# A hybrid decoder layer on one core: sample-scan products laid between z products, sample sequences as attention units, the last conv tap on ScalarE, the last down tiles block by block

## What is computed

```python
h = rms_norm(x); z, xBC, dt, q, k, v, g1, g2 = split(h @ w_in)
u = silu(causal_conv4(xBC)); y = ssd_scan(u, dt, state) * silu(z)        # 32 heads of 64, 8 groups, state 128
A = group_norm(y) @ w_ssm_out;  B = window_attention_with_sinks(rope(q), rope(k), v) @ w_attn_out
x = x + (sigmoid(g1) * A + sigmoid(g2) * B) @ w_out
x = x + peer(rms_norm(x))     # 16384 experts, 8 heads, top 16: sum of gate * gelu(h . u_e) * v_e
y = rms_norm(x)               # also: new conv rows, new scan states, new k and v windows
```

## Time and profile before

| | us |
|---|---|
| median of 3 runs | 2764.11 (2760.47 to 2771.31) |
| the profiled execution | 2769.13 |
| its span | 2767.3 |
| conv stage, middle | 60.0 to 249.5 |
| sample scan with z tiles | 398.4 to 614.1 |
| prompt attention | 694.4 to 824.1 |
| sample attention | 824.1 to 875.4 |
| down tiles | 2010.0 to 2740.7 |
| behind the last down tile | 2740.7 to 2767.3 |

### The profile page before, as it was taken

The page is one execution under the profiler, slowest core; times in us unless marked ns, Lnnn a source line. Parts: engine busy times, 40 slices in busy tenths (PEclk is TensorE's granted clock), DMA queues, the critical chain, the costliest instruction groups (busy, mean ns, idle before and its releaser), DMA issues.

```text
span 2767.3 us, 45108 instructions
## 1 busy us (share of the span) xinstructions
PE 2539.8 (92%) x14964; PEld 2329.5 (84%) x14964; DVE 1932.9 (70%) x3510; ACT 1032.8 (37%) x1975; POOL 963.6 (35%) x540
## 2 busy tenths in 40 slices
PE   6999679999768999989999998998998999999997
PEld 5998469999436999979988888888898999999996
DVE  5998864543663752238899998888566888888876
ACT  2332752226332532113333387787332222222221
POOL 1333353323000333324445565656432222222221
PEclk9999887899886999989999999999999999999999
DMA  3222243332001222313334478788899999999994
GB/s 128 70 81 70 87 137 105 113 116 79 28 6 31 68 77 83 106 52 115 122 130 142 142 260 295 258 316 298 322 315 311 311 308 312 313 304 312 312 302 150
DMA packets 264994, 490.31 MB, mean 177 GB/s; under 512 B 137249, under 2 KB 172833, under 8 KB 263713
## 3 DMA queue, kind: packets, MB, share of 16 engines
q1 hardware_dynamic: 67408, 222.85, 23.7%
q10 hardware_dynamic: 160624, 132.00, 14.7%
q0 software_dynamic: 36864, 134.23, 13.8%
HBM read 417.59 MB, written 73.39 MB: 177 GB/s over the span
## 4 chain that ended last, share of the span: by engine, by line
PE 38%; DVE 8%; DMA 3%; ACT 3%; issue 2%; POOL 1%; ACTq 1%; DVEq 0%; SPq 0%
PE ps L1132 23%; PE ps L1031 11%; PE ps L654 2%; DMA raw<-wt 2%; PE ps L1102 1%; DMA row<-pu,row_idx 1%; DVE onehot_pick L2173 1%; POOL wlo L565 1%; ACT rinv L1553 1%; DVE onehot_pick L2170 1%; DVE expert_parts L2176 1%; ACT g_block L1572 1%; ACT whi L1197 1%; ACT onehot_i L1557 1%; DVE pick L2150 0%
## 5 line engine op out<-in xcount | busy, mean ns | idle before, releaser
L565 POOL TENSOR_TENSOR wlo<-raw,whi 128x1024 fp32r<-128x1024 f32 x215 | 547.1, 2545 | 1077.5 <-ACT whi L1197 1077.3
L1197 ACT ACTIVATE whi<-raw 128x1024 fp32r<-128x1024 f32 x373 | 394.5, 1058 | 1346.0 <-PE ps L1132 461.0
L1031 PE MATMUL ps<-h_hi,whi 128*128 128x448 f32 x1024 | 382.3, 373 | 15.9 <-POOL wlo L565 10.8
L1132 PE MATMUL ps<-act_hi,whi 128*128 128x448 f32 x1024 | 374.8, 366 | 8.7 <-DVE act_lo L1643 8.7
L1031 PE MATMUL ps<-h_lo,whi 128*128 128x448 f32 x1024 | 378.4, 370 | 0.0
L1031 PE MATMUL ps<-h_hi,wlo 128*128 128x448 f32 x1024 | 377.9, 369 | 0.0
L1132 PE MATMUL ps<-act_lo,whi 128*128 128x448 f32 x1024 | 374.6, 366 | 0.0
L1132 PE MATMUL ps<-act_hi,wlo 128*128 128x448 f32 x1024 | 374.6, 366 | 0.0
L572 POOL DMA_INDIRECT row<-pv,row_idx x128 | 163.0, 1273 | 471.6 <-DVE row_acc L2253 459.7
L2246 DVE TENSOR_TENSOR wlo<-raw,whi 128x1024 fp32r<-128x1024 f32 x158 | 193.7, 1226 | 130.0 <-ACT whi L1197 122.3
L654 PE MATMUL ps<-h_hi,whi 128*128 128x288 f32 x1104 | 249.1, 308 | 27.6 <-DVE h_lo L1643 19.7
(11 more groups left out here) (309 smaller groups left out, 4687.5 us busy)
## 6 DMA issues: line engine op xcount, KB each, us to landing
raw<-wt SPq DMA_DIRECT2D x245, 512.0 KB, 3.4
raw<-pv SPq DMA_DIRECT2D x128, 512.0 KB, 6.1
activations<-tmp ACTq DMA_DIRECT2D x128, 224.0 KB, 2.4
gates_dense<-g_block ACTq DMA_DIRECT2D x7, 4096.0 KB, 15.5
g_tile<-gates_dense ACTq DMA_DIRECT2D x128, 224.0 KB, 5.2
gelu<-activations ACTq DMA_DIRECT2D x128, 224.0 KB, 5.5
a_cum_rows<-decay_sums SPq DMA_DIRECT2D x32, 256.0 KB, 3.1
state_s<-s_in SPq DMA_DIRECT2D x16, 512.0 KB, 4.7
```

Of the source, the lines that this page charges most:

```text
L565: pool.tensor_tensor(lo, raw[n.par][:, :], hi.bitcast(F32), ALU.subtract).then_inc(split_ready, 1)
L1031: mm = pe.matmul(PS[2 * p.par][:, 0:DT], w[slot][:, k, :], x[:, k, 0:DT], start=k == 0 and w is whi and x is HH, stop=k == KD - 1 and w is ...
L1132: mm = pe.matmul(PS[d][:, 0:DT], w[s][:, d, :], x[b][:, :], start=first and w is whi and x is ACH, stop=last and w is wlo)
L1197: act.activation(whi[slot][:, :, :].rearrange("p k c -> p (k c)"), raw[slot][:, :], ACT.Copy)\
```

## The change

It has four parts.

1. *Sample scan.* `past` and `new_states` become `past_part` and `new_part`, one product each, and `project_z` issues one of them behind each of the first two of the three passes of every k: 16 in a z tile. z tile 0 carries past 0, z tile 2g+1 past g+1, z tile 2g+2 new states g, z tile 15 new states 7. ACT's, DVE's, POOL's and SP's orders are laid anew around it (`z_tile(0)` in front, `back_sample` and `yz` ahead of `front(u+1)`; two weight tiles loaded per two states).
2. *Sample attention.* Two sequences form a unit u = 16 to 19 of the prompt's pipeline (UA = 20 units). q is staged for all eight at once, all caches have buffers of their own and are loaded by SP behind `v_tok`, and SP stores the windows. The next stage's first tile waits for `sc_used`, and `o_done` is awaited ahead of the second.
3. *Conv.* ACT writes tap 3 and the bias from PSUM into `conv_acc` (two Identity activations of 288 columns); DVE adds taps 0 to 2.
4. *End.* The last three down tiles are done block by block; adds, squares and a sum of squares on DVE follow each block; the row sums are turned behind block 5; PE sums the squares in 8 + 2 products; ACT weighs X with the final weight, and the last multiplication is split between DVE (6) and POOL (2).

```diff
-            def past(g):
-
-                pe.wait_ge(y_used, PU + g - 2)
-                for w in range(2):
-                    v = 2 * g + w
+            def past_part(g, i):
+
+                w, b = divmod(i, SB)
+                v, lo = 2 * g + w, 256 + P * w + SL * b
+                if i == 0:
+                    pe.wait_ge(y_used, PU + g - 2)
+                if b == 0:
                     pe.wait_ge(s0_in[v % 8], 16 * (v // 8 + 1))
-                    for b in range(SB):
-                        lo = 256 + P * w + SL * b
-                        mm = pe.matmul(bank(PU + g)[:, lo:lo + SL], S0[v % 8][:, b, :],
-                                       UBS[:, NG + g, SL * b:SL * (b + 1)], start=True, stop=True)
+                mm = pe.matmul(bank(PU + g)[:, lo:lo + SL], S0[v % 8][:, b, :],
+                               UBS[:, NG + g, SL * b:SL * (b + 1)], start=True, stop=True)
+                if b == SB - 1:
                     mm.then_inc(off_ready, 1)
 
-            def new_states(g, w):
-
-                for half in range(2):
-                    q = 4 * g + 2 * w + half
-                    if q >= 2:
-                        pe.wait_ge(cs_used, q - 1)
-                    for b in range(4):
-                        mm = pe.matmul(PS[(7, 1)[half]][:, b * P:(b + 1) * P],
-                                       BMS[g % 2][0:NS, 4 * half + b, :],
-                                       XDD[0:NS, (2 * g + w) * P:(2 * g + w + 1) * P], start=True, stop=True)
+            def new_part(g, i):
+
+                w, half, b = i // 8, i // 4 % 2, i % 4
+                q = 4 * g + 2 * w + half
+                if i == 0:
+                    pe.wait_ge(x_taken, (PU + g) // 2 + 1)
+                    pe.wait_ge(bms_ready, g + 1)
+                if b == 0 and q >= 2:
+                    pe.wait_ge(cs_used, q - 1)
+                mm = pe.matmul(PS[(7, 1)[half]][:, b * P:(b + 1) * P], BMS[g % 2][0:NS, 4 * half + b, :],
+                               XDD[0:NS, (2 * g + w) * P:(2 * g + w + 1) * P], start=True, stop=True)
+                if b == 3:
                     mm.then_inc(cs_ready, 1)
 
-            def project_z(m):
+            def project_z(m, past=None, new=None):
 
                 n = Idx(N_Z + m)
                 slot = slot_of(n)
@@ -802,37 +836,34 @@
                 if m:
                     pe.wait_ge(zs_ready, m)
                 for k in range(KD):
-                    for w, x in ((whi, HH), (whi, HL), (wlo, HH)):
+                    for i, (w, x) in enumerate(((whi, HH), (whi, HL), (wlo, HH))):
                         for h in range(2):
                             mm = pe.matmul(PS[2 + h][:, 0:HT], w[slot][:, k, :], x[:, k, h * HT:(h + 1) * HT],
-                                           start=k == 0 and w is whi and x is HH,
-                                           stop=k == KD - 1 and w is wlo)
-                mm.then_inc(tile_done, 1)
+                                           start=k == 0 and i == 0, stop=k == KD - 1 and i == 2)
+                        if i == 2 and k == KD - 1:
+                            mm.then_inc(tile_done, 1)
+                        if i < 2:
+                            if past is not None:
+                                past_part(past, 2 * k + i)
+                            if new is not None:
+                                new_part(new, 2 * k + i)
...
-                if 0 < g < NG - 1:
-                    past(g + 1)
-                    scores_cb(u + 1)
-                pe.wait_ge(x_taken, u // 2 + 1)
-                pe.wait_ge(bms_ready, g + 1)
-                new_states(g, 0)
                 pe.wait_ge(mt_ready, u + 1)
-                if g == 0:
-                    past(0)
-                project_z(2 * g)
                 for r in range(4):
                     h = 4 * g + r
                     out = bank(u)[64 * (r % 2):64 * (r % 2) + 64, P * (r // 2):P * (r // 2) + NS]
                     mm = pe.matmul(out, XDT[0:NS, h * HP:(h + 1) * HP], SEG[u % 2][0:NS, r, 0:NS],
                                    start=True, stop=True)
                 mm.then_inc(y_ready, 1)
-                if g == 0:
-                    past(1)
+                if g < NG - 1:
+                    project_z(2 * g + 1, past=g + 1)
                     scores_cb(u + 1)
-                new_states(g, 1)
-                project_z(2 * g + 1)
+                    project_z(2 * g + 2, new=g)
+                else:
+                    project_z(2 * g + 1, new=g)
...
+            project_z(0, past=0)
...
-            for u in range(UNITS):
+            for u in range(UA):
                 turn(u)
-                if u < UNITS - 2:
+                if u < UA - 2:
                     scores(u + 2)
                 values(u)
...
+            def last_block(d):
+
+                for j in range(1, 4):
+                    s = slot_of(Idx(N_ALL - 4 + j))
+                    for w, x in ((whi, ACH), (whi, ACL), (wlo, ACH)):
+                        mm = pe.matmul(PS[d][:, 0:DT], w[s][:, d, :], x[j][:, :], start=False,
+                                       stop=j == 3 and w is wlo)
+                mm.then_inc(sums_ready, 1)
+
+
+            pe.wait_ge(split_ready, N_ALL)
+            pe.wait_ge(act_ready, ET)
+            for d in range(KD):
+                last_block(d)
+                if d == 5:
+
+                    pe.wait_ge(rows_done, 1)
+                    pe.wait_ge(added, 4)
+                    for k in range(KD):
+                        mm = pe.transpose(PS[2 + k // 4][:, k % 4 * P:(k % 4 + 1) * P], ACCS[:, k * P:(k + 1) * P],
+                                          ident)
+                    mm.then_inc(rows_turned, 1)
+            pe.wait_ge(tok_std, 1)
             for k in range(KD):
-                mm = pe.transpose(PS[k // 4][:, k % 4 * P:(k % 4 + 1) * P], ACCS[:, k * P:(k + 1) * P], ident)
-            mm.then_inc(rows_turned, 1)
-            square_sums(2)
+                mm = pe.matmul(PS[1][:, 0:P], ONES[:, :], SQF[:, k, DT:T], start=k == 0, stop=k == KD - 1)
+            mm.then_inc(row_sum, 1)
+            pe.wait_ge(sq_summed, 1)
+            pe.matmul(PS[0][:, 0:DT], ONES[:, :], SQF[:, 0, 0:DT], start=True, stop=False)
+            pe.wait_ge(sqf_ready, KD)
+            pe.matmul(PS[0][:, 0:DT], ONES[:, :], SQF[:, KD - 1, 0:DT], start=False, stop=True).then_inc(dense_sum, 1)
...
+                if not first:
+                    act.wait_ge(silu_done, m - 1)
+                for h in range(2):
+                    ins = act.activation(CO[k][:, h * HT:(h + 1) * HT], (lo, hi)[h][:, 0:HT], ACT.Identity,
+                                         bias=Q[:, bass.ds(m + Q_CB, 1)], scale=Q[:, bass.ds(m * 4 + (Q_CW + 3), 1)])
+                ins.then_inc(slot_used[n.par], 1)
...
+                    z_tile(0)
                 if u < SU - 1:
                     exps(u + 1)
                 if u >= PU:
-                    z_tile(2 * (u - PU))
+                    z_tile(2 * (u - PU) + 1)
                 if u % 2 and u // 2 + 2 < NC * 4:
                     take_b(u // 2 + 2)
-                if u >= PU:
-                    z_tile(2 * (u - PU) + 1)
+                if u >= PU and u < SU - 1:
+                    z_tile(2 * (u - PU) + 2)
...
+            def weigh(k):
+
+                act.activation(YO[:, k, :], X[:, k, :], ACT.Copy, scale=Q[:, Q_FIN + k:Q_FIN + k + 1])\
+                    .then_inc(scaled, 1)
+
+            def square_dense(d):
+                act.wait_ge(added, d + 1)
+                act.activation(SQF[:, d, 0:DT], X[:, d, 0:DT], ACT.Square).then_inc(sqf_ready, 1)
+
+            for d in range(6):
+                square_dense(d)
+            act.wait_ge(rows_added, 1)
+            act.activation(SQF[:, :, DT:T], X[:, :, DT:T], ACT.Square).then_inc(tok_std, 1)
+            for k in range(3):
+                weigh(k)
+            for d in (KD - 2, KD - 1):
+                square_dense(d)
+            for k in range(3, 6):
+                weigh(k)
+            act.wait_ge(row_sum, 1)
+            act.activation(TMP[0][:, DT:T], PS[1][:, 0:P], ACT.Sqrt, bias=Q[:, Q_EPS:Q_EPS + 1], scale=1.0 / D)
+            act.wait_ge(dense_sum, 1)
+            act.activation(TMP[0][:, 0:DT], PS[0][:, 0:DT], ACT.Sqrt, bias=Q[:, Q_EPS:Q_EPS + 1],
+                           scale=1.0 / D).then_inc(std_ready, 1)
+            for k in range(6, KD):
+                weigh(k)
             for k in range(KD):
-                act.wait_ge(y_done, k + 3)
+                act.wait_ge(y_half if k % 3 == 2 else y_done, k // 3 + 1 if k % 3 == 2 else k - k // 3 + 1)
...
-                for tap in range(1, 4):
+                for tap in range(3):
...
+                back_sample(g)
+                yz(2 * g)
                 if g < NG - 1:
                     front(u + 1)
-                add_states(g, 0)
-                back_sample(g)
-                yz(2 * g)
                 if g % 2 == 0 and u // 2 + 2 < NC * 4:
```

(12 more changed lines are left out.)

346 lines of the change are left out of this document (162 added, 184 removed).

## The result

The changed kernel takes **2932.19 us** (median of 4 runs, 2916.36 to 2936.19) against 2765.52 before (4 runs): 1.0591 times as long, 95% interval 1.0547 to 1.0636. The span grew from 2767.3 to 2929.1, by 161.8 us.

What follows compares the result with a forecast made beforehand. PE, busy in 92% of the span, was taken as the bound, losing by waits and low clock. Scan +24, attention -17.5, conv -3, end -6 sum to -2.5, giving 2762 us from the median 2764.11; range 2728 to 2806.

Steps and rivals of the forecast that it cites:

- (a): Scan: whether bare waits of 3.3 us drop the clock; eight drops before new-state tiles, wide work restoring it, +16 us.
- The other end that I had kept for this (+84): Scan: upper bound if all eight new-state tiles stay at half clock to their end, 8 x 10.5 us.
- rival 2: Scan: mixed past tiles read as idle, half clock, 9.9 us each; 2782 (four) to 2821 (eight) us; chance 0.20.
- The sum: Scan's products at full clock: z 102, new states 33, past 28, others about 5, together 168 us.
- 9.9 and 10.5: Scan: full-clock us of a past tile and of a new-state tile, taken as the extra cost at half clock.
- (b): Scan: whether a past tile of wide and tiny products holds the clock; mostly, with two tiles low, +20 us.
- rival 1: Scan: the clock is never lost or is back at once; scan 204 to 219, whole 2726 to 2741 us; chance 0.30.
- the hindered end of 4.4 to 7.2: End: last multiplications on DVE beside POOL, 4.4 us if they do not hinder each other, 7.2 if they do.
- The 0.75 for not slower: Whole kernel: chance of a time not slower than 2778 us; slower was given 0.25.

Runs made afterwards that it cites:

- the later kernel: The changed kernel with eight small products ahead of each boundary wait, eight behind k=3, and Silu ahead of high part: 2698.00 us; with conv as before 2726.67 us.

## Why the prediction was wrong

**Part 1, the scan, the new-state tile.** The step that failed is (a): "about 4 us of half clock until wide work restores it costs 2 us, so +16". It took the new-state tile for a place where the clock recovers, from z products that had been dense. In the changed kernel it recovers in none of eight (0.50 in each), and each costs some 28 us of products in place of the 12.5 forecast (10.5 and 2 of half clock). The other end that I had kept for this (+84) was the right one, and I gave the question to the past tiles instead, as rival 2 does. The eight past tiles at half were the consequence: they mostly keep what the new-state tiles hand them, and with 128 rows in the new-state products four of the eight are at 1.00.

**The price of a single new-state product.** The sum priced it at 0.128 us from a run of sixteen, where 64-row products follow one another. I did not look at the weight loads. The trace of before has the opening on both sides of such a run, at half clock behind it and at full clock ahead of it:

```profile
426.42 0.50 PEld L807 LDWEIGHTS ps<-h_hi,whi 128*128 128x128 f32 x2 [0.22 <-issue]
...
594.78 1.86 PEld L792 LDWEIGHTS ps<-xdt_decayed,b_by_seq 64*128 64x128 f32 x16 [0.16 <-issue]
```

Once per run that is nothing; 32 times per tile, at 0.16 to 0.22, it would have been an estimated 5 to 7 us a tile, 41 to 56 in all. It measured 9.1 us a tile at half clock, 73 in all, and worse, in the kernel without it the clock came back. This is the missing term of the sum. The Trainium skill, "TensorE: Matmul & The Clock Gate", Part 2 (Step-by-step: what each phase is for), says that the weights of the next product load while the present one runs, if the row groups do not conflict or the load goes to the background buffer. The trace agrees where 128 rows follow 128 (no idle time before the loads around a new-state product over 128 rows). At the change to 64 rows and back 0.28 and 0.22 us stood open; which of the page's conditions failed there no run shows.

**Half clock is not double time.** The rivals doubled 9.9 and 10.5. By the earlier trace rows a z instruction goes from 0.133 to 0.24, 1.8 times. All at half the products took 314 us against 168, 1.87 times. That made the upper ends some 20 us too high, which hid part of the missing term.

**The waits.** 28.5 against 36, with a longest of 2.9 against 3.1: right in kind, the measured sum a fifth lower. Whether a wait of 3 us at full clock drops it was answered by the kernel with 128 rows: in its trace all three waits of 3.00 us in front of a new-state tile after a tile at 1.00 led to some 3 to 4 us of 0.50. Of its seven waits of 1.02 to 1.46, three were followed by a fall as well, and each of those past tiles then stayed low to its end. So (a) had the drop right; what it missed was the recovery. (Prompt attention before has four waits of 3.30 us and one of 2.72, where the prediction speaks of five of 3.3; slow products followed all of them.)

**The past tile (b).** That it "mostly holds, but not in each tile" is what such a tile does by itself: with 128 rows in the other tiles four of eight were low, two were forecast. At full clock it takes 10.4 us with its small neighbours, forecast 9.9. I had not thought of a tile that runs at either level, so nothing in the sum said what happens when the tiles between never give full speed back.

**The clock and busy time.** The changed kernel's scan had PE busy in 385.32 of 415.61 us and a clock of 0.50 throughout. The rule of the Trainium skill that rival 1 rested on ("TensorE: Matmul & The Clock Gate", Part 1, The HAM clock gate: idle lowers, busy restores) would have had it rise in the first tile, if busy is read as a profile counts it. What the experiments leave open is whether the clock reacted to the open loads or to the 64-row products among wide ones; runs of eight 64-row products let it recover, so the open loads are the likelier. That is an argument; no kernel had one without the other, and the cause stays open at this depth.

**Part 2, sample attention.** -17.5 forecast, 175.78 - 156.69 = -19.1 measured, inside the ends of -15 and -20. PE's idle time over all of attention fell from 49.8 to 31.8 us, and its clock was 0.77 against 0.74: the step holds.

**Part 3, conv.** -3 forecast, with -7 as the end; -13.4 measured and confirmed by undoing it. The step that failed is "What a faster DVE can return is the wait where conv drains: 2.9 us". It took PE's 184.3 of 189.5 for a floor and priced that wait without the half clock behind it. The starts of the same products in the two traces tell where the time went. After six conv tiles the changed kernel is 2.8 us ahead: before, PE waited 4.2 us for a low part until 77, and the clock was at 0.50 until 82; now it waits 2.9 us and keeps 1.00. The next 24 tiles bring 3.3 more. Then comes the wait of the earlier trace rows:

```profile
252.84 0.64 PE L699 MATMUL ps<-consts_sb,da_tok 128*32 128x128 f32 x2 [2.89 <-DVE da_by_seq L1730]
```

Its going brings 2.4. Behind it the clock had been at 0.50 from 253 to 266, and the decay sums took 8.3 us; now they take 4.8 at full clock, 3.5 more. The wait for the last Silu fell from 5.6 to 3.6, the last 1.7. (With conv as before in the later kernel the clock is low there again, from 254 to 267.)

For the middle tiles the chain of DVE is the likely bound. In the kernel before:

```profile
200.38 2.52 POOL L565 TENSOR_TENSOR wlo<-raw,whi 128x1024 fp32r<-128x1024 f32 x1 [4.19 <-ACT whi L1197]
```

```profile
200.68 2.30 DVE L1708 SCALAR_TENSOR_TENSOR conv_acc<-conv_in_s,params_sb,conv_acc 128x64 f32<-128x64 f32 x1
...
203.68 0.28 DVE L1708 SCALAR_TENSOR_TENSOR conv_acc<-conv_in_s,params_sb,conv_acc 128x64 f32<-128x64 f32 x1
```

and in the changed kernel, conv's middle by groups:

```profile
L1751 DVE SCALAR_TENSOR_TENSOR conv_acc<-conv_in_s,params_sb,conv_acc 128x64 f32<-128x64 f32 x71 | 20.1, 283 | 1.7
```

The same instruction takes 0.28 us alone and 2.30 while POOL makes a low part, so two microseconds of each tile were a stop, not work. Now POOL's low part falls mostly into DVE's wait for ACT, and its tail into the copy behind that wait (0.59 to 0.66 us in place of 0.18). The tap's mean fell from 1007 to 283 ns. From 100 to 220 us PE went from 883 to 902 instructions, 2% of that stretch. The Trainium skill, "GPSIMD Engine Reference", 1. Specifications, has POOL share its SBUF interfaces with VectorE, in contention with VectorE instructions in a two-port mode or with two SBUF inputs. The trace agrees for the sample tap, which has two.

**Part 4, the end.** -6 forecast, -5.4 measured; 0.8 of it only moved, since the transposes of the row sums now stand among the down products. The reciprocal began 6.3 us behind the down products (2914.14 against 2907.86), forecast 6.7, or 5.7 by the sum's own times (2747.4 less 2741.7). The six multiplications took 6.55, near the hindered end of 4.4 to 7.2.

**The rivals.** Rival 2 had the sign and the kind (a mixed tile in which the clock stays low) with a chance of 0.20; its place was wrong. Its last line, new-state tiles low as well at 2889, lies 43 us under the result. In the scan it lies 49 under (367 against 415.6): the 73 of the open loads, less the 20 doubled too much and the 8 of waits, come to 45. The other parts gained 11 more than summed, and the traced executions differ by 6 less than the medians. The 0.75 for not slower rested on the recovery of a tile that the trace of before did not have, and on a price from a run.

## What to carry to other kernels

When single products of one shape are laid between those of another, price them as singles among the others, and not from a run of their own: a change in the number of contraction rows cost 0.28 us at half clock, and with 64 rows padded to 128 by zeros this kernel took 2754 us in place of 2932. Ask of every mixed stretch whether the clock can rise in it, and not only whether it falls: this one was busy at half speed for all of its 415 us. Price a wait together with the half clock behind it: in conv a wait of 2.9 us had 3.5 more behind it. In this kernel small products were worth most as a cover ahead of the wait at a tile's boundary, in runs of eight, with the function that frees the banks first in ACT's order.
